# Filler products in TensorE's waits, and one modulation block loaded to a ninth weight slot, in a two-layer diffusion block

## The reference

```python
sh1, sc1, g1, sh2, sc2, g2 = split(silu(c) @ w_mod[l] + b_mod[l])    # the same for the context
u = rms_norm(h, norm1_g[l]) * (1 + sc1) + sh1
y = token_mixers(u, uc, w_in[l], ...)       # neighbourhood, conv, GQA and differential attention
h = h + g1 * (y @ w_out[l])
u = rms_norm(h, norm2_g[l]) * (1 + sc2) + sh2
aff = softmax(u @ w_router[l])              # 16 experts
g, idx = top_k(aff.T, cap)                  # 64 latent tokens of each expert, 32 of the context
xe = u[idx]
y = (silu(xe @ w_gate) * (xe @ w_up)) @ w_down
h = h + g2 * scatter_add(idx, y * g)
```

## Time and profile before

| | us |
|---|---|
| median of three runs | 2093.96 (2091.21 to 2098.76) |
| the profiled execution, its time | 2102.55 |
| its span, on which the rows' times are | 2100.7 |
| TensorE busy | 1945.5 (93%) |
| VectorE, ScalarE, GpSimd busy | 675.8, 507.7, 343.7 |
| granted TensorE clock, mean over the span | 0.97 of full |

### The profile page before, as it was taken

How to read it: one execution, slowest core, us unless ns; L and a number is a source line. 1 busy time by engine, 2 the same in 40 slices (tenths; PEclk the granted TensorE clock), 3 DMA queues, 4 the chain that set the end, 5 groups by cost and what they waited for, 6 DMA issues and landing times.

```text
span 2100.7 us, 40920 instructions
## 1 busy us (share of the span) xinstructions
PE 1945.5 (93%) x18270; PEld 1270.0 (60%) x18270; DVE 675.8 (32%) x1327; ACT 507.7 (24%) x1124; POOL 343.7 (16%) x200
## 2 busy tenths in 40 slices
PE   6999999989879999999999999999994999998897
PEld 4656667655546666767666655667742666655554
DVE  3075367762530000000001416368735011111112
ACT  4001236650401111211111310236612111110112
POOL 0004037740000111001100005037700000000000
PEclk9999999999989999999999799999997999999998
DMA  9431150041499999999997312110046899999995
GB/s 399 169 150 41 40 201 1 2 161 40 165 370 424 402 401 412 408 405 401 403 376 307 136 65 73 43 41 1 1 160 255 335 427 426 426 426 426 427 427 231
DMA packets 44779, 525.48 MB, mean 250 GB/s; under 512 B 5248, under 2 KB 6272, under 8 KB 14528
## 3 DMA queue, kind: packets, MB, share of 16 engines
q1 hardware_dynamic: 36176, 492.21, 56.8%
q0 software_dynamic: 6992, 25.43, 3.8%
q10 hardware_dynamic: 1440, 5.24, 0.6%
HBM read 506.88 MB, written 15.99 MB: 249 GB/s over the span
## 4 chain that ended last, share of the span: by engine, by line
PE 71%; DMA 11%; DVE 5%; issue 5%; PEld 3%; POOL 2%; ACT 2%; ACTq 0%; SPq 0%; DVEq 0%; PEldq 0%; POOLq 0%
PE ps L968 14%; PE ps L633 12%; PE ps L962 9%; PE ps L974 7%; PE ps L834 7%; PE ps L651 4%; DMA arena<-in_w_exp 4%; PE ps L771 4%; PE ps L794 2%; PE ps L1029 2%; PE ps L810 2%; DMA u<-in_w_exp 2%; DMA ring<-in_w_exp 2%; POOL arena L1882 2%; PEld ps L962 1%
## 5 line engine op out<-in xcount | busy, mean ns | idle before, releaser
L633 PE MATMUL ps<-u,ring 128*128 128x512 f32 (+1 forms) x800 | 276.9, 507 | 0.0
L1882 POOL TENSOR_SCALAR arena<-arena,rsum 128x768 f32<-128x768 f32 (+3 forms) x120 | 216.5, 1819 | 277.3 <-DVE rsum L1670 226.3
L633 PEld LDWEIGHTS ps<-u,ring 128*128 128x128 f32 x800 | 151.7, 190 | 123.3 <-issue 115.2
L1801 DVE SCALAR_TENSOR_TENSOR arena<-arena,ps 128x512 f32<-128x512 f32 x40 | 27.4, 684 | 541.0 <-ACT arena L1350 541.0
L968 PE MATMUL ps<-ring,arena 128*32 128x256 f32 x3200 | 185.2, 383 | 6.0 <-PE ps L974 4.3
L962 PE MATMUL ps<-ring,arena 128*64 128x256 f32 x1376 | 157.9, 385 | 9.8 <-DMA ring<-in_w_exp 5.8
L962 PE MATMUL ps<-arena 128*64 128x256 f32 x1344 | 151.7, 380 | 12.0 <-ACT arena L1358 6.5
L968 PEld LDWEIGHTS ps<-ring,arena 128*32 128x32 f32 x3200 | 118.9, 111 | 63.6 <-issue 14.2
L1274 ACT ACTIVATE arena<-arena,negmax 128x768 f32<-128x768 f32 (+3 forms) x160 | 129.8, 812 | 96.1 <-DVE arena L1650 74.9
L962 PEld LDWEIGHTS ps<-ring,arena 128*64 128x64 f32 x1376 | 103.1, 139 | 61.2 <-DMA ring<-in_w_exp 11.4
L834 PE MATMUL ps<-u,ring 128*128 128x512 f32 (+1 forms) x384 | 137.8, 521 | 0.0
(11 more groups left out here) (217 smaller groups left out, 2325.5 us busy)
## 6 DMA issues: line engine op xcount, KB each, us to landing
ring<-in_w_exp SPq DMA_DIRECT2D x93, 2048.0 KB, 25.2
arena<-in_w_exp SPq DMA_DIRECT2D x78, 2048.0 KB, 27.6
ring<-in_w_mod SPq DMA_DIRECT2D x20, 2048.0 KB, 11.8
u<-in_w_exp SPq DMA_DIRECT2D x20, 2048.0 KB
ring<-in_w_in SPq DMA_DIRECT2D x10, 2048.0 KB, 15.5
ring<-in_w_out SPq DMA_DIRECT2D x4, 2048.0 KB, 8.1
arena<-in_w_mod SPq DMA_DIRECT2D x4, 2048.0 KB, 7.8
u_rows<-arena ACTq DMA_DIRECT2D x10, 512.0 KB, 3.0
```

The costliest lines, as they stand in the source:

```text
L633: mm = pe.matmul(ps[:, bb, 0:n], w[:, k, P * ct:P * ct + P], u[:, k, t0:t0 + n], start=k == 0, stop=k == KD - 1)
L1882: pool.tensor_scalar(e0, e0, rsum[:, c0:c0 + 1], None, ALU.mult).then_inc(s["p_norm"], 1)
```

## The change

There are two parts. The first adds `keep_clock(n, bank)`: n matmuls of the identity with 512 constant columns into a bank of PSUM whose content nobody needs at that point. It is called in ten places, 41 products in all: in layer 0 before the first block of the input projection (2), before attention (2), before the first gather (6) and before `y_back` is awaited (3), where the wait for `e_xev` moves ahead of it; in layer 1 before and behind each of two `spread`s (4 times 1), before the ranks are awaited (18) and before the first gather (6). The second part changes the slots of layer 0's modulation blocks 21, 22 and 23 from 4, 5, 0 to 8, 4, 5, with a wait of SyncE for `n2_pre` before slot 8 is filled.

```diff
-        SLOTS = [[0, 1, 2, 3] * 3 + [0, 1, 2, 3, 0, 2, 3, 0, 2, 3, 1, 4, 5, 0, 2, 3, 1, 4, 5, 0], [0, 2, 3, 1, 0, 2, 3, 1]]
+        SLOTS = [[0, 1, 2, 3] * 3 + [0, 1, 2, 3, 0, 2, 3, 0, 2, 3, 1, 4, 5, 0, 2, 3, 1, 8, 4, 5], [0, 2, 3, 1, 0, 2, 3, 1]]
...
+                    if key[0] == "mod" and slot_of[at[key]] == 8:
+                        sp.wait_ge(sig["n2_pre", 0], 2 * KD)
...
+            def keep_clock(n, bank=0):
+                for x in range(n):
+                    pe.matmul(ps[:, bank, :], cst("ident"), const[:, 0:512], start=True, stop=True)
...
                     modulation(range(4))
+                    keep_clock(2, 7)
                 else:
                     pe.wait_ge(sig["e_acc", 0], FILLS + KD)
+                    keep_clock(1, 7)
                     pe.wait_ge(sig["n1_inv", l], 1)
                     spread(TL + TC).then_inc(sig["n1_rb", l], 1)
+                    keep_clock(1, 7)
...
                 pe.wait_ge(sig["v_ev", l], since("v_ev", l) + nv)
+                if l == 0:
+                    keep_clock(2, 3)
                 pe.wait_ge(sig["rp_add", l], since("rp_add", l) + 7)
...
                 if l:
+                    keep_clock(1, 2)
                     pe.wait_ge(sig["n2_inv", l], 1)
                     spread(TL).then_inc(sig["n2_rb", l], 1)
+                    keep_clock(1, 2)
...
+                if not both:
+                    keep_clock(18)
                 pe.wait_ge(sig["r_rank", l], since("r_rank", l) + 1)
...
                     if n == 0:
+                        pe.wait_ge(sig["e_xev", l], 4 * PAIRS)
+                        keep_clock(3, 7)
                         pe.wait_ge(sig["y_back"], 16 * (TL + TC))
-                        pe.wait_ge(sig["e_xev", l], 4 * PAIRS)
...
+                keep_clock(6)
                 gather(0, 0)
```

## The result

Twenty runs of each kernel: the changed kernel took 2090.23 us in the median (2085.61 to 2099.22), the kernel before 2097.36 (2087.13 to 2101.71). The ratio is 0.9977, with a 95% interval from 0.9966 to 0.9988, so the change is worth some 4.8 us, between 2.5 and 7.1. Forecast were 15.3 us, and 2078.7 us; 2090.23 lies above the range.

The account below looks back on a forecast made before the run. The prediction took TensorE to bound layer 0's experts and DMA layer 1's. Its terms, 0.7 + 1.5 + 4.9 + 4.2 - 1.6 + 1.5 + 0 + 0.4 + 3.7 = 15.3 us, off 2093.96 gave 2078.7 us, range 2071 to 2088.

Parts of the forecast that it names:

- What bounds layer 0's experts: Layer 0's expert products: TensorE, busy 516.07 of 522.5 us, sets the stage, so an earlier or faster TensorE ends it earlier.
- give-back of 1.6 us: End of layer 0: `y_back`, issued 9.1 us earlier, lands only 7.5 us earlier, so 1.6 us of gains are lost.
- The clock at layer 0's first gather: Layer 0's first gather: transposes gain 1.4 us and the first 128 expert products 2.8 at the high clock; 4.2 together.
- The clock is 1.00 from there on: Sign: the granted clock stays at 1.00 from layer 0's first gather on; the first 128 expert products take 6.9 us.
- Layer 0's slot: Layer 0's modulation blocks: block 21 loads in a DMA hole, so the first gather lands one block earlier; gain 4.9 us.
- a sign of being wrong: Layer 0's first gather starting more than 2 us later than said would show the prediction wrong.
- Layer 0's start and attention: Layer 0's first projection and attention: products behind the waits run at the high clock; gains 0.7 and 1.5 us.
- Behind y_back: End of layer 0: three products fit the 4.3 us wait; transposes and products behind it run faster, gaining 1.5 us.
- Layer 1's start: Layer 1's start: 1.0 us lost to a filler, up to 1.2 saved by the clock; taken as 0.
- Layer 1's norm and router: Layer 1's second norm gains 0.4 us; transposes and first expert block behind the router's fillers gain 3.7 us.
- the clock does not hold: Rival, chance 0.15: fillers too few to hold the high clock; 2085.2 us, or 2090.1 if only the slot is left.
- the gather was to land before 604: Layer 0's first gather: rings taking turns packet by packet would land it before 604, the sum taking 5.9 for 4.9.

Follow-up runs that it names:

- e15: e5 repeated unchanged; 2086.22 us, ratio 0.9935 to the kernel before.
- e7: The change with eight idle products between layer 0's first gather and the first experts' products; 2083.85 us, one run.
- e13: e5 with the last weight block of layer 0's experts held until `y_back` landed, and four fillers for nine there; 2080.69 us, ratio 0.9913.
- e14: e13 with the last two weight blocks of layer 0's experts held instead of one; 2080.87 us, ratio 0.9915.
- e16: e13 with layer 1's tenth block also held until the first gather landed, and six fillers for nine ahead of that gather; 2076.38 us, ratio 0.9897.
- e17: e13 repeated unchanged; 2079.48 us, ratio 0.9912 to the kernel before.
- e3: The change with one filler within and one behind each layer's first gather, nine for six ahead of layer 1's; 2085.88 us, ratio 0.9951.
- e1: The kernel before with the slot change alone, no fillers; 2093.07 us, ratio 0.9978.
- e5: e3 with nine fillers for three ahead of `y_back`; 2081.92 us, ratio 0.9925.
- e11: The kernel before with the slot change and nine fillers ahead of `y_back`, no others; 2090.52 us, ratio 0.9984.
- e2: The kernel before with the 41 filler products alone, slots as before; 2095.45 us, ratio 0.9991.
- e8: e5 with one idle product behind each of the later thin sums ahead of layer 1; 2087.57 us, ratio 0.9958.

## Why the prediction was wrong, point by point

**What bounds layer 0's experts.** Here it failed. "That stage is set by TensorE" was read from 516.07 busy us of 522.5 and the absence of waits for weights. The stage ends with `y_back`, and what sets `y_back` is that the weights' bytes are through: (c) stayed within 531.5 and 533.8 us in 15 profiles, whether TensorE was 2.9 us ahead of the change (e15) or 6.0 us behind it (e7), and fell below 529.1 only when weights were held (e13, e14, e16, e17). The full DMA share of 1.01 was in the same row, and the prediction named it, but as a give-back of 1.6 us only. The change kept 0.4 us of (c) where 2.6 were forecast (4.2 - 1.6). `y_back` landed 5.2 us earlier, near the lower of the two bounds that the prediction gave (4.9 and 9.1), not at the 7.5 that it chose between them.

**The clock at layer 0's first gather** (4.2). The transposes gave about 1.4, the 128 products nothing (9.97 us). "The clock is 1.00 from there on" failed: the fillers stood ahead of the gather, and the clock fell again during the thin work and short waits within it. With products within the gather the clock held in e15 and dipped in e3, and the 128 products ran fast in both; by (c) that is worth 0 to 1.4 us, because of the first point.

**Layer 0's slot** (4.9): right in mechanism and nearly in size, 4.5 us in (b), at the time and place that were named, and as much in the timings of e1 as the whole change gave. By the means of all profiles it is 4.1 us: 18.5 in the three with the old slots (18.7, 17.8, 18.9), 14.4 in the sixteen with the new. The gather still lands behind two expert blocks; its transposes began at 605.13 where 603 was forecast, just over the 2 us that the prediction had named as a sign of being wrong.

**Layer 0's start and attention** (2.2): right. The attention's 1.5 is seen where it was forecast (1.93 us for 3.43), the first projection's 32 instructions took 8.7 us for 9.19 (0.5 where 0.7 was forecast), and (a) is 2.1 us shorter in the mean, though the change's own (a) shows only 0.3: single profiles differ by more.

**Behind y_back** (+1.5): it was -1.4. The three products were sized for the wait of before, 4.3 us; the wait grew to 5.11 us beyond their end, since TensorE was 8.8 us earlier and `y_back` only 5.2. That 3 us of idle time would be left was forecast; that the clock falls in them was not. With nine products (e5) the same two steps took 4.7 us, less than the forecast 4.75: the size was right, the number of products was not.

**Layer 1's start** (0): undecided. (d) is 50.6 or 59.6 us in one and the same kernel without fillers, 51.0 to 57.4 in the code of the change, 47.4 to 59.6 elsewhere. Whether the products shift the odds can't be told from so few profiles.

**Layer 1's norm and router** (0.4 + 3.7): about 0, (e) 46.7 and 48.9 for 47.4 and 46.6. The ranks came 29.2 us behind the router's first product for 30.4 (29.2 in all 13 profiles with the single products, 29.2 to 30.4 in the 6 without); the gather gave that back, as it lands behind the weights, not behind the ranks. The six products then ended 2.63 us ahead of it, the clock fell at 1615.3, and the first block ran at it. The term had taken the gather's 4.6 us as its own pace, which was right (4.40), and left out what it would meet when it starts earlier. With nine products, one within and one behind (e3 and on) the clock held and 2 to 3 us of the 3.7 came; with the tenth block held, 2.1 more. So the step that failed here is the overlap: the six products were sized on the 6.06 us of before.

**The sum.** 2.1 + 4.5 + 0.4 - 1.4 + 0 = 5.6 us, with layer 1's start left out, against 4.8 measured (2.5 to 7.1). This sum mixes means and single profiles, and its terms are known to about 1 us each, so that it comes close is partly luck. Of the 9.4 us forecast for the clock at the gather, at `y_back` and in layer 1's router (4.2 + 1.5 + 3.7), next to nothing reached the end. Of the rivals, "the clock does not hold" was nearest: for the case that nothing holds but the slot it gave 2090.1 us, against 2090.23, and the Trainium skill's "HAM oscillation" ("TensorE: Matmul & The Clock Gate"), cited for it, is borne out at the gather, at `y_back` and at layer 1's router. But it was given 0.15, and the range's upper end lay below it.

The other rule cited, turns between the rings packet by packet ("DMA: Bandwidth & Descriptors", on arbitration of the Trainium skill), fits roughly with the count of packets during `y_back` (440 to 358, if the profile's packets are the rule's) and does not promise equal bytes: the packets differ by a factor of 3.8. In layer 1's gather 25 packets stood against 993, which turns of single packets do not give; no run here tells why. By the rule the gather was to land before 604, and it landed at 605.1, though only 0.02 MB of weights moved between 603 and then: the measurement decides.

**The base.** The three runs lay 3.4 us below the median of twenty, and the profile 5.2 us above. Of the 11.5 us by which the forecast missed, 3.4 are the base and 8.2 the gain (15.3 less the 7.1 between the medians).

## What to carry to other kernels

Before an engine is called the bound of a stage, look at what the stage's last wait is released by, and what is queued ahead of that transfer; a full DMA share (1.01 here) beside a busy TensorE is a reason to ask whether a lead of TensorE is worth anything; here it was worth 0 to 1.4 us of 2.9. Small transfers on another queue, issued behind weights, landed here only about when the weights were through: holding one block that was not needed yet (two lines on SyncE, twice) gave 4 and 2 us in the profiles, more than all the idle products of the change. Fillers have to reach to the end of a wait and not beyond it (three were too few at `y_back`, nine too many in e11), and to stand within thin work behind it, and a stretch at the low clock in one profile may not be in the next: compare two profiles of one kernel before a stretch is priced. The best kernel here, e16_hold_tenth, takes 2076.38 us, 0.9897 (0.9874 to 0.9921) of the kernel before.

## What the runs showed of the hardware that was not expected

The mean granted clock says little of the time. Over the timed runs it was 0.985 in the change and 0.972 in the kernel before (the 30 runs beside e1); e2, with the fillers alone, had 0.984 and was 0.9991 of before, so most of the clock that was won seems to lie in waits, or in work that nothing waited for. Within one kernel it tells much: the change's twenty runs go from 0.990 (2085.66 us) to 0.981 (2099.22 us), the longer runs mostly at the lower clock. That fits the two profiles of the kernel before, which differ by 9.1 us in span and by 9.0 us in (d).

A transfer's time from issue to landing is no property of the transfer: layer 1's first gather took 4.40, 4.6 and 6.77 us, and the last part of `y_back` 25.4 us (e7), 27.07 (before) and 31.3 (e8), or 21.3 us once two weight blocks were held (e14).
